# Attention heads unrolled, scores in three passes of split tiles, and the compressed stage in one pass

## The reference

```python
# even mixer: 8 NSA heads in 2 groups, 8 dilated heads, head width 64
s_c = einsum(q, kc) * scale             # kc, vc: 31 compressed keys and values a group
o_c = _probs(s_c, cmp_end <= t) @ vc
...                                     # top_k(imp, 8 of 8 blocks): every causal key
o_s = softmax(q @ ks * scale, causal) @ vs
o_w = softmax(q @ kw * scale, causal) @ vw
out = g[0] * o_c + g[1] * o_s + g[2] * o_w
# dilated heads: three branches, merged by their log-sum-exp, causal
# latent mixer: 16 heads, q and k of width 64 + 32, v of width 64
sc = (qn @ k_nope + qr @ k_rope) * 96 ** -0.5
o  = softmax(sc, causal) @ v
# full attention: 8 query heads, 2 key heads of width 128, 512 queries, 512 + 256 keys
o  = softmax(q @ k * 128 ** -0.5) @ v
```

## Time and profile before

| | |
|---|---|
| median of 3 runs | 3901.3 us (3901.02 to 3901.65) |
| the profiled execution | 3896.48 us |
| its span | 3894.7 us |
| mean granted TensorE clock in it | 0.925 of 2.4 GHz |
| TensorE, VectorE, ScalarE busy | 89%, 53%, 32% |
| compressed stage | 47.6 us |
| NSA and dilated heads | 185.0 us |
| latent heads | 118.2 us |
| full attention | 156.7 us |

### The profile page before, as it was taken

The page is one execution under the profiler, slowest core; times in us unless marked ns, Lnnn a source line. Parts: engine busy times, 40 slices in busy tenths (PEclk is TensorE's granted clock), DMA queues, the critical chain, the costliest instruction groups (busy, mean ns, idle before and its releaser), DMA issues.

```text
span 3894.7 us, 47690 instructions
## 1 busy us (share of the span) xinstructions
PE 3483.3 (89%) x16433; PEld 2822.0 (72%) x16433; DVE 2051.7 (53%) x2953; ACT 1229.4 (32%) x1890; POOL 271.5 (7%) x258
## 2 busy tenths in 40 slices
PE   8999988889999999988999994498899875778999
PEld 6888767567888788865678883398688753566887
DVE  7743433555753675355555435675655356335553
ACT  3222311443222322233532222454333232323332
POOL 1000111001000100022010003300000011000000
PEclk9999995999999999888999997599899987998999
DMA  5533240003542354211045420265233210012332
GB/s 170 171 94 98 88 109 1 0 7 112 168 124 81 109 171 124 81 59 33 1 118 167 124 92 27 59 172 163 76 97 102 91 65 22 1 43 76 97 103 70
DMA packets 390883, 347.27 MB, mean 89 GB/s; under 512 B 11344, under 2 KB 343437, under 8 KB 390669
## 3 DMA queue, kind: packets, MB, share of 16 engines
q1 hardware_dynamic: 390797, 346.16, 29.8%
HBM read 344.02 MB, written 2.10 MB: 89 GB/s over the span
## 4 chain that ended last, share of the span: by engine, by line
PE 77%; DVE 12%; issue 4%; ACT 3%; POOL 2%; SPq 1%; DMA 0%; DVEq 0%; ACTq 0%; POOLq 0%
PE ps L759 22%; PE ps L760 22%; PE ps L761 22%; PE ps L850 3%; PE ps L824 2%; POOL sq_sum L2147 2%; PE ps L1244 1%; ACT w_hi L1297 1%; DVE w_lo L1310 1%; DVE a_lo L1635 1%; DVE rstd L1658 1%; PE ps L841 1%; DVE x_T L2131 1%; PE ps L821 1%; PE ps L957 1%
## 5 line engine op out<-in xcount | busy, mean ns | idle before, releaser
L759 PE MATMUL ps<-a_hi,w_hi 128*128 128x512 f32 (+1 forms) x2968 | 1144.7, 386 | 135.5 <-DVE a_lo L1901 42.7
L760 PE MATMUL ps<-a_lo,w_hi 128*128 128x512 f32 (+1 forms) x2968 | 1130.6, 381 | 0.0
L761 PE MATMUL ps<-a_hi,w_lo 128*128 128x512 f32 (+1 forms) x2968 | 1130.0, 381 | 0.0
L759 PEld LDWEIGHTS ps<-a_hi,w_hi 128*128 128x128 f32 x2968 | 570.8, 192 | 281.4 <-issue 114.6
L1310 DVE TENSOR_TENSOR w_lo<-w_raw,w_hi 128x1024 fp32r<-128x1024 f32 (+1 forms) x536 | 636.3, 1215 | 183.3 <-ACT w_hi L1297 169.4
L1297 ACT ACTIVATE w_hi<-w_raw 128x1024 fp32r<-128x1024 f32 (+1 forms) x536 | 549.8, 1044 | 308.5 <-PE ps L761 306.7
L761 PEld LDWEIGHTS ps<-a_hi,w_lo 128*128 128x128 f32 x2968 | 571.6, 193 | 103.8
L760 PEld LDWEIGHTS ps<-a_lo,w_hi 128*128 128x128 f32 x2968 | 572.5, 193 | 100.8 <-issue 1.0
L759 PE MATMUL ps<-hs_hi,w_hi 128*128 128x512 f32 (+1 forms) x1232 | 464.9, 377 | 2.8 <-DVE w_lo L1310 1.5
L760 PE MATMUL ps<-hs_lo,w_hi 128*128 128x512 f32 (+1 forms) x1232 | 463.7, 376 | 0.0
L761 PE MATMUL ps<-hs_hi,w_lo 128*128 128x512 f32 (+1 forms) x1232 | 463.3, 376 | 0.0
(11 more groups left out here) (250 smaller groups left out, 3251.5 us busy)
## 6 DMA issues: line engine op xcount, KB each, us to landing
w_raw<-in_ffn_w_up SPq DMA_DIRECT2D x220, 512.0 KB, 4.8
w_raw<-in_ffn_w_down SPq DMA_DIRECT2D x154, 512.0 KB, 3.5
ada_raw<-in_ada_w SPq DMA_DIRECT2D x96, 512.0 KB, 3.9
w_raw<-in_ffn_w_gate SPq DMA_DIRECT2D x88, 512.0 KB, 5.1
w_raw<-in_ev_w_in SPq DMA_DIRECT2D x20, 512.0 KB, 3.6
w_raw<-in_attn_w_qkv SPq DMA_DIRECT2D x16, 512.0 KB, 4.2
w_raw<-in_ev_w_out SPq DMA_DIRECT2D x8, 512.0 KB, 4.1
w_raw<-in_mla_w_out SPq DMA_DIRECT2D x8, 512.0 KB, 3.2
```

The lines of the kernel that those rows point to most:

```text
L759: mm(dst, hi, rhi, start=start, stop=False)
L760: mm(dst, hi, rlo, start=False, stop=False)
L761: return mm(dst, lo, rhi, start=False, stop=stop)
```

## The change

- The loops over groups of four heads become straight code over all heads of a run. The scores of head u + 1 are threaded through head u for every u, and the first transpose of head u + 1 is issued ahead of the last values of head u.
- ScalarE's order in a head becomes take, exponential, exponential, take and so on (full attention: take, exponential in each quarter). VectorE's order is as before within a head.
- q and k are split in high and low tiles, and scores are three f32r matmuls. The high part is a ScalarE copy (`qk_hi`), the low a VectorE subtraction (`qk_lo`). Some tiles are split ahead of the attention, the others as `later[u]`: on ScalarE behind head u's exponentials, on VectorE ahead of `finish(u)`. NSA: 7 of 14 tiles in the rotary stage, one in each of heads 0 to 6 (these 7 are for the dilated heads). Latent: heads 0 and 1 ahead, then the two tiles of head u + 2 in head u. Full: four tiles ahead, then one in each of heads 0 to 5.
- The staging copies of GpSimd and their zeros are gone. An even head reads its 64 rows of q and k directly.
- q is scaled by minus the softmax's scale ahead (in the eviction, the norm's gain or the head gain), so the scores are negated, the masks change sign, VectorE takes a minimum, and ScalarE uses it as bias with scale -1. `NM` (L1690) is gone.
- The compressed stage is one pass over 8 heads: 16 three-pass score matmuls 64 wide (both groups' keys side by side), VectorE and ScalarE work on 512 columns, 8 transposes of 128 x 128, 8 value matmuls 256 wide against a block-diagonal `vc`, 8 outputs. `kc` is split, `vc` and the hidden layer of the values are made in four copies.

```diff
             def attention(at):
...
-                    turn_(0)
-                    for j in range(per_t):
-                        if u < 3 and j % (per_t // 4) == 0:
-                            scores(u + 1, it, (j // (per_t // 4),))
-                        if j + 1 < per_t:
-                            turn_(j + 1)
-                        values(j)
-                with pe.Fori(0, at.units // 4) as it:
-                    scores(0, it)
-                    for u in range(4):
-                        rest(u, it)
+                def scores(u, c):
+                    head = at.heads[u]
+                    if c == 0 and head["need"] is not None:
+                        pe.wait_ge(qk_lo_s.sem, head["need"])
...
+                            last = three(dst, q[0], q[1], k[0], k[1], True, True)
...
+                for u in range(at.units):
+                    if u == 0:
+                        turn_(0, 0)
+                    for j in range(per_t):
+                        if u + 1 < at.units and j % (per_t // 4) == 0:
+                            scores(u + 1, j // (per_t // 4))
+                        if j + 1 < per_t:
+                            turn_(u, j + 1)
+                        elif u + 1 < at.units:
+                            turn_(u + 1, 0)
+                        values(u, j)
...
+            def qk_hi(split):
+                do(split[1], split[0], ACT.Copy).then_inc(qk_hi_s.sem, 1)
...
+                for u in range(at.units):
+                    more = u + 1 < at.units
+                    for j in range(1, per_t, 2):
+                        take(u, j)
+                        for c in ((j // 2,) if full else (j - 1, j)) if more else ():
+                            exps(u + 1, c)
+                    for split in at.later[u] if u < len(at.later) else ():
+                        qk_hi(split)
...
+            def qk_lo(split, n):
+                src, hi, lo = split
+                dve.wait_ge(qk_hi_s.sem, n + 1)
+                v.tensor_tensor(lo, src, hi.bitcast(F32), ALU.subtract).then_inc(qk_lo_s.sem, 1)
...
+                for u in range(at.units):
+                    more = u + 1 < at.units
+                    for j in range(0, per_t, 2):
+                        take(u, j)
+                        for c in ((j // 2,) if full else (j, j + 1)) if more else ():
+                            maxima(u + 1, c)
+                    for split in at.later[u] if u < len(at.later) else ():
+                        qk_lo(split, split0 + nsplit[0])
+                        nsplit[0] += 1
+                    finish(u)
...
+                    for it in range(4):
+                        for c in range(4):
+                            tok = slice(c * P, (c + 1) * P)
+                            dst = ps[:, it // 2, :].rearrange("p (i s c n) -> p i s c n", i=2, s=2, c=4)[:, it % 2, :, c, :]
+                            last = three(dst, F_hi(it)[:, tok], F_r[:, it, tok], kc_hi[:, :], kc_lo[:, :], True, True)
...
+                        for h in range(4):
+                            mm(ps[:, 4 + 2 * i + h // 2, 256 * (h % 2):256 * (h % 2) + 256], cmp_pT[:, 4 * i + h, :], vc[:, h % 2, :],
+                               start=True, stop=True).then_inc(pv_s.sem, 1)
...
-            def stage_queries(at):
...
-                        g.tensor_copy(stage[rows, u, :].unsqueeze(1), q[rows]).then_inc(st_s.sem, 1)
```

More of the change, by code:

```diff
@@ L158, in __init__ @@
     def __init__(self, kind, first=0, n=0, half=0, norm=None, stream=None, mod=None, layer=None, wg=None, wu=None, wd=None,
-                 xT=None, x_sig=None, T=None, xin=0, units=0, full=False, per_t=0, stages=0, steps=0, tab_in=0, scale=1.0,
-                 work=None, mask=None, kind_=None, rows=P, dim=0, o=None, q=None, k=None, v=None, out_at=None, ada=None):
+                 xT=None, x_sig=None, T=None, xin=0, units=0, full=False, per_t=0, tab_in=0, work=None, mask=None, dim=0, heads=None,
+                 later=(), ada=None):
         self.kind = kind
@@ L455, in even_phase @@
+            ph.qk0 = qk_hi_s.plan(len(SPLIT))
+            qk_lo_s.plan(len(SPLIT))
             ph.cmp = Phase("cmp")
[L456 to L463, removed]
-                                    v=lambda it, u, kb: v_tok[:, kb, u // 2, HD * (u % 2):HD * (u % 2) + HD])
@@ new lines, in even_phase @@
+            ph.nsa = attention_plan(heads, "causal", work=work_even, mask=masks[:, 0, :], dim=HD,
+                                    later=[[(F[:, f, :], F_hi(f), F_r[:, f, :])] for f in SPLIT[7:]])
+            heads = []
+            for i in range(4):
+                for side in range(2):
+                    h = 2 * i + side
+                    heads.append(head(11 + i, 15 + i, side,
+                                      lambda kb, i=i, s=side: v_tok[:, kb, 2 + i, HD * s:HD * s + HD],
+                                      o_tok[:, :, 512 + h * HD:512 + h * HD + HD], len(SPLIT)))
@@ L471, in even_phase @@
+            ph.dil = attention_plan(heads, "causal", work=work_even, mask=masks[:, 1, :], dim=HD)
             out_plan(ph, a_hi, a_lo)
@@ new lines, in values @@
+                def values(u, j):
+                    c, kbs = units_t[j]
+                    made, first = ((ptd_s, at.ptd0), (pta_s, at.pta0))[j % 2]
+                    pe.wait_ge(made.sem, first + per_t // 2 * u + j // 2 + 1)
+                    if j == 0 and u >= 2:
+                        pe.wait_ge(o_s.sem, at.o0 + u - 1)
+                    for i, kb in enumerate(kbs):
+                        last = mm(ps[:, 6 + u % 2, c * D:(c + 1) * D], wk.pT[:, j % 2, i * P:(i + 1) * P],
+                                  at.heads[u]["v"](kb), start=(kb == 0), stop=(kb == (5 if full else c)))
+                    last.then_inc(pv_s.sem, 1)
@@ L1543, in _ @@
                     values(3)
+                    act.wait_ge(rd_s.sem, ph.rd0 + 12)
+                    for split in ph.first_splits:
+                        qk_hi(split)
                     attention(ph.att)
```

551 lines of the change are left out of this document (282 added, 269 removed).

## The result

The changed kernel takes 3991.58 us (median of 4 runs, 3981.85 to 3994.22) against 3901.16: 1.0228 times the time before, with a 95% interval of 1.021 to 1.0245, so 90 us slower. The forecast was 3963, with a range of 3888 to 3995. The profiled execution has a span of 3992.4 against 3894.7, and I account for that difference of 97.7; it is 7 more than that of the medians, as the profiled execution is the longest of the changed kernel, and before it was shorter than the median.

A forecast was written before the change was run, and what follows sets the result against it. TensorE was taken as the bound: busy 89% of the span, 77% of the last chain. Terms -26.5 + 79 + 50 - 42 + 1 = +61.5 on 3896.5 gave 3958, plus 4.8 for the median: 3963 us, range 3888 to 3995.

The forecast's parts named there:

- The clock in the even mixer: 24 even heads: without bursts and filled rows they stay at 1.2 GHz; +79 us, bounds -10 to +85.
- Rival (a): Even and latent heads: the clock comes back as before, whole kernel 3850 us; chance 0.14.
- TensorE's own work in a head at 0.50: Cold even head: scores 3.2 us, ten transposes and twenty value matmuls 6.4, together 9.6.
- the chain: End of a causal head: maxima, exponential, splits, output, take, values in series; cold even heads 12.1 split, 10.9 unsplit, 10.1 dilated.
- The compressed stage: Compressed stage: one pass in two groups of about 21.5 us replaces four turns; -26.5 us, within 3 either way.
- The latent mixer: 16 latent heads: splits lengthen each head's end and the clock is mostly cold; +50 us, between +16 and +70.
- Full attention: Full attention: take ahead of the exponential, a quarter falls from 5.02 to about 3.0 us; -42, between -30 and -47.
- The rest: Small extras: gain columns, scaled reciprocals, split copies in the rotary stage; +1 us, from 0 to 2.5.

## Why the prediction was right

**The clock in the even mixer** (+79, measured +91.5) was the step that decided the sign, and the runs show it as argued: filled rows. The rows alone give back 106 us; fillers on 128 rows bring the clock up in both runs of heads, and the same on 32 rows leave it at 0.50 but for one stretch of 13.7 us. Not all of the 106 is the clock: a part is the steps between 64 and 128 rows, 1.44 a head at 0.50. One sentence of mine was wrong in detail: the heads didn't start at 0.50. The clock had come up within the new compressed stage's 128-row values, and was gone after the first 64-row head, 13.7 us later. Rival (a) thus needed not only a rise but a hold. What spoke for it was work nearly unbroken; by that alone the latent heads with 32-row fillers, 200.00 us unbroken, should have run at 1.00, and they stood at 0.50.

**The size of it** was short by 12.5, past the +85 that I had given as its bound. (My own terms give 258.6 - 178.4 = 80.2, not 79.) The term is TensorE's own work in a head at 0.50, which I had at 9.6: scores 3.2 from the columns, 3 x 1280 at 1.2 a ns, and 6.4. From the timeline the four tiles of scores take 0.83, 0.94, 1.25 and 1.58 (872.33 to 873.16, 874.09 to 875.03, 876.61 to 877.86, 880.08 to 881.66), 4.6. The unbroken latent head with splits at mid-head tells two things apart. It takes 9.90, 0.3 above my 9.6: passes of 64, 128 and 256 columns all take 0.213 at 0.50, and that is 0.3 more for the 128-wide tile than its columns. The 1.44 from there to the dilated head's 11.34 is the change between 64 and 128 rows, for which I had nothing in the sum. With both the heads came out at 11.34 in place of 10.1 (dilated), 11.51 in place of 10.9 and 12.54 in place of 12.1 (NSA): they rose by less than 1.7, since what I had put on the chain, 0.5, 1.3 and 2.5, was too much, and that is an error of the other sign.

**The compressed stage** (-26.5, measured -20.7, outside the 3 either way that I gave) has the same floor in it: 24 passes a group of 64 columns were to take 2.6 us at 0.107; they take 5.1, as the timeline of the changed kernel shows by the starts of the first three, 0.21 to 0.23 apart:

```profile
637.47 0.42 PE L812 MATMUL ps<-kc_hi,F_r 128*128 128x64 f32 x1 [1.28 <-DVE vc L1899]
637.70 0.40 PE L813 MATMUL ps<-kc_lo,F_r 128*128 128x64 f32 x1
637.92 0.40 PE L814 MATMUL ps<-kc_hi,F_r 128*128 128x64 f32 x1
```
I had halved the spacing of an f32 value record with the argument that it covers two passes. No run shows that for a width of 64: the record and the pass both take 0.213 at 0.50; a record takes twice the pass at 256 columns (0.427 and 0.213) and at 512 (0.853 and 0.427). And the second group's passes, which I had hidden, are on the path:

```profile
647.95 0.69 DVE L1918 SCALAR_TENSOR_TENSOR cmp_p<-ps,cmp_add 128x512 f32<-128x512 f32 x1 [2.90 <-PE ps L814]
...
650.01 0.68 DVE L1927 TENSOR_TENSOR cmp_p<-cmp_p,cmp_keep 128x512 f32<-128x512 f32 x1
```

VectorE's mask of the first group (650.01), whose exponential is done at 645.7, is queued behind three steps of the second, the first of which waits for that group's 24 passes. Ahead of the first pass stand 4.8 us more, the last part of them the four copies of `vc`. Against that the values ran partly at 1.00, from 657.7 on.

**The latent mixer** (+50, between +16 and +70, measured +61.2). Both parts are there: the chain (11.77 a cold split head, forecast 11.8; at full clock 8.18 with the fillers in its hole, forecast 8.41) and the clock at 0.56 over the run. Mid-head splits separate them: 31 us are the chain with what it does to the clock, and f32 scores take 57 away. The forecast put the cold clock on broken and shorter work. Shorter work is shown: without the holes of the splits the clock still stood mostly at 0.50, with TensorE 46.00 of 46 us busy in one stretch, and with f32 it rose and held. What the holes add to it isn't separated here, but they count on 128 rows, where the even heads' clock flickered with holes of 2.76 (0.82 in that window) and not with 0.67 (1.00). The 11.8 is partly luck: TensorE's own work in a cold head is 9.90 and not 9.6, and the hole 1.67.

**Full attention** (-42, measured -43.0): a quarter of 3.05 (two starts of its scores in the timeline of the changed kernel, below), split heads of 13.72 to 13.85 behind a first one of 14.22, against 13.9.

```profile
3459.18 0.48 PE L812 MATMUL ps<-k_att_hi,q_att_hi 128*128 128x512 f32 x1
...
3462.23 0.48 PE L812 MATMUL ps<-k_att_hi,q_att_hi 128*128 128x512 f32 x1
```

The reason, the take ahead of the exponential, is shown by the order alone in the kernel before.

**The rest** (+1, measured +8.7) was too small. One part is plain: scores wait for the splits ahead of the latent run, 2.1 us from the end of the rotary work where 1.1 had passed, and 2.6 against 1.1 in full attention. The other 6 lie elsewhere between the stages, among them the heads' end at 0.50, after which the clock came up only at 941. I didn't resolve them.

The errors are +5.8, +12.5, +11.2, -1.0 and +7.7, together the 36 by which the profiled spans differ from the forecast sum of +61.5. Four of five went the same way, three stages lie outside the bounds that I gave them, and the median is only 3.4 us under the upper end of the range: the path was right, and that the range held the sum was in part luck.

## What to carry to other kernels

Before narrowing a matmul's contraction from 128 rows to 64, look at the granted clock of its stage and not at its matmul count: an operand padded with zeros can be faster than the half that it replaces, by the clock and by the steps between the two widths. Here a dilated head with f32 scores took 6.05 us on 128 rows, half of them zeros, at 1.00, and 12.19 on 64 rows at 0.50; at an equal clock the transpose came 0.56 behind a pass on 64 rows, and 0.43 behind one on 96. Where a stage with a busy TensorE stands at 0.50, a few useless full-row matmuls in a gap are a cheap test, and full rows for the real work were the better cure here (3794.75 against 3877.95). Try the order of two instructions on one engine by itself before building a large change around it.

## What the runs showed that I had not expected

TensorE ran 200 us without a pause at 0.50 when its work filled 32 to 128 rows in turn. Near the edge the clock is a coin toss: with four fillers one binary gave 3845 to 3899. Between passes on 64 rows and matmuls on 128 the weight load didn't run ahead, and a head of the same columns took 1.44 us longer at 0.50 (11.34 and 9.90). And an f32r pass at 0.50 took 0.213 us at 64, 128 and 256 columns alike (637.70 to 637.92, 872.60 to 872.81 and 874.47 to 874.69 in the changed kernel), so there a pass isn't paid by its columns; at 1.00 one of 128 took 0.11. What sets that floor no run tells.
